# Opening modulation of a fused two-stage network: the 8 MiB matrix in two column halves, six buffers, its first product tiles started early, and later loads for other inputs

## The reference, cut to what matters

```python
def first_block(x, c, w_ada, b_ada, g_norm1, w_in, ...):
    ada = (c @ w_ada + b_ada)[:, None, :]               # c: (1, 1024), w_ada: (1024, 6144)
    shift1, scale1, gate1, shift2, scale2, gate2 = jnp.split(ada, 6, axis=-1)
    h = rmsnorm(x, g_norm1) * (1.0 + scale1) + shift1
    proj = h @ w_in                                     # all projections of the attention block
    (q_f, k_f, v_f, f_logit, q_d, k_d, v_d, q_i, k_i, w_i,
     gate_fox, gate_dsa) = jnp.split(proj, SPLIT_POINTS, axis=-1)
    log_f = jax.nn.log_sigmoid((f_logit + b_forget).astype(jnp.float32))
    cum_logf = jnp.cumsum(log_f, axis=1)
    ...                                                 # two attentions, gates, output product
    x = x + gate1 * (merged @ w_out)
    h2 = rmsnorm(x, g_norm2) * (1.0 + scale2) + shift2
    x = x + gate2 * (jnp.square(jax.nn.relu(h2 @ w_mlp1)) @ w_mlp2)
    return rmsnorm(x, g_final)
```

## Time and profile before

| what | value |
|---|---|
| median of three executions | 1395.11 us |
| the profiled execution | 1397.11 us |
| its span in the trace | 1395.4 us |
| TensorE busy | 1341.5 us, 96% of the span |
| VectorE, ScalarE, GpSimd busy | 823.8, 660.1, 79.6 us |
| read from HBM | 266.21 MB, 192 GB/s over the span |

### The profile page before, as it was taken

One profiled execution on the slowest core, in us unless ns is written; L12 is line 12 of the kernel. 1 busy time (PEld: TensorE's weight loads), 2 busy tenths in 40 slices (PEclk: granted clock), 3 DMA queues, 4 the chain that ended last, 5 costly groups with the idle time before them and its releaser, 6 DMA issues.

```text
span 1395.4 us, 16274 instructions
## 1 busy us (share of the span) xinstructions
PE 1341.5 (96%) x6233; PEld 1099.6 (79%) x6233; DVE 823.8 (59%) x1118; ACT 660.1 (47%) x1054; POOL 79.6 (6%) x114
## 2 busy tenths in 40 slices
PE   2999999999999999999989999999999999999997
PEld 2788877788888788888768888887888888888885
DVE  5686767867565654556437654557554575755454
ACT  2665555553444543445655443444443444544442
POOL 3400100100001000001001000000000010100000
PEclk9999999999999999999999999999999999999999
DMA  9766654458454655546424655557556555665551
GB/s 337 248 228 224 219 204 160 172 181 312 141 206 156 211 184 209 181 181 207 173 104 124 218 195 186 182 180 226 181 199 193 181 197 176 193 203 194 173 195 56
DMA packets 156717, 268.38 MB, mean 192 GB/s; under 512 B 9477, under 2 KB 101717, under 8 KB 155616
## 3 DMA queue, kind: packets, MB, share of 16 engines
q1 hardware_dynamic: 148896, 239.43, 50.3%
q0 software_dynamic: 7744, 27.91, 6.1%
HBM read 266.21 MB, written 1.07 MB: 192 GB/s over the span
## 4 chain that ended last, share of the span: by engine, by line
PE 87%; DVE 5%; DMA 3%; ACT 2%; POOL 1%; issue 1%; SPq 0%; DVEq 0%; ACTq 0%; POOLq 0%
PE UP L672 17%; PE UP L674 16%; PE UP L673 16%; PE Y L672 10%; PE Y L674 10%; PE Y L673 10%; PE TB L743 4%; DVE WL L1386 2%; DMA RAW<-in_w_in 1%; DMA X<-in_x 1%; POOL RS L599 1%; POOL VAR L598 1%; PE Y L773 1%; PE Y L780 1%; ACT WH L1047 1%
## 5 line engine op out<-in xcount | busy, mean ns | idle before, releaser
L1386 DVE TENSOR_TENSOR WL<-RAW,WH 128x1024 fp32r<-128x1024 f32 (+2 forms) x446 | 512.3, 1194 | 180.3 <-ACT WH L1047 174.1
L1047 ACT CAST WH<-RAW 128x1024 fp32r<-128x1024 f32 (+2 forms) x446 | 433.7, 1031 | 215.5 <-PE Y L674 126.1
L672 PE MATMUL UP<-WH,AH 128*128 128x512 f32 (+1 forms) x1120 | 452.0, 404 | 5.2 <-DVE WL L1386 3.3
L674 PE MATMUL UP<-WH,AL 128*128 128x512 f32 (+1 forms) x1120 | 437.9, 391 | 0.0
L673 PE MATMUL UP<-WL,AH 128*128 128x512 f32 (+1 forms) x1120 | 436.7, 390 | 0.0
L672 PEld LDWEIGHTS UP<-WH,AH 128*128 128x128 f32 x1120 | 211.3, 189 | 50.7 <-issue 8.5
L674 PEld LDWEIGHTS UP<-WH,AL 128*128 128x128 f32 x1120 | 210.9, 188 | 44.3
L673 PEld LDWEIGHTS UP<-WL,AH 128*128 128x128 f32 x1120 | 211.6, 189 | 39.6 <-issue 0.5
L672 PE MATMUL Y<-WH,HH 128*128 128x512 f32 (+1 forms) x496 | 193.8, 391 | 0.0
L674 PE MATMUL Y<-WH,HL 128*128 128x512 f32 (+1 forms) x496 | 191.8, 387 | 0.0
L673 PE MATMUL Y<-WL,HH 128*128 128x512 f32 (+1 forms) x496 | 191.7, 387 | 0.0
(11 more groups left out here) (213 smaller groups left out, 925.5 us busy)
## 6 DMA issues: line engine op xcount, KB each, us to landing
RAW<-in_ffn_w_gu SPq DMA_DIRECT2D x176, 512.0 KB, 5.0
RAW<-in_ffn_w_down SPq DMA_DIRECT2D x80, 512.0 KB, 4.1
RAW<-in_w_mlp SPq DMA_DIRECT2D x64, 512.0 KB, 4.2
RAW<-in_w_in SPq DMA_DIRECT2D x38, 512.0 KB, 5.9
PIECE<-in_w_ada POOLq DMA_DIRECT2D x32, 512.0 KB, 5.4
RAW<-in_a_w_in SPq DMA_DIRECT2D x24, 512.0 KB, 4.6
WADA<-in_w_ada SPq DMA_DIRECT2D x7, 1024.0 KB, 10.0
RAW<-in_w_out SPq DMA_DIRECT2D x8, 512.0 KB, 3.8
```

The lines of the kernel that those rows point to most:

```text
L672: pe.matmul(dst, ah, wh, start=first, stop=False)
L674: return pe.matmul(dst, al, wh, start=False, stop=last)
L1047: act.copy(WH[:, u % 2, q * n:(q + 1) * n], raw_half(u, q // 2)[:, (q % 2) * n:(q % 2 + 1) * n]).then_inc(wh_done, 1)
L1386: ve.tensor_tensor(WL[:, u % 2, o], raw_half(u, q // 2)[:, (q % 2) * n:(q % 2 + 1) * n], WH[:, u % 2, o].bitcast(F32), ALU.subtract).then_ ...
```

## The change

1. `w_ada` is loaded in column halves: a pair is two row blocks by 512 columns of shift and 512 of scale (two DMAs, 1 MiB). Four pairs make half 0, four half 1. Six places: the four of `WADA` and two in `ADA`. SP's order is now pair 0 of half 0, `x`, three pairs, unit 0, four pairs of half 1, unit 1. In the kernel before it was `w_ada` blocks 0 to 3, `x`, blocks 4 to 7, unit 0, unit 1.
2. ScalarE does the first product of each half (`opening_product`), VectorE adds the others in 512-column instructions, two for each row block, into `TG` (half 0) and `TMP` (half 1). The last two of half 1 are cut to 256 columns.
3. TensorE sums by quarters (two channel tiles), and unit 0 runs quarter by quarter for both token blocks (`first_unit`), into `Y[1]` instead of `UP`. Products whose result nobody reads stand between (`keep_busy`: 8, 6, 16 and 6 of 384 columns).
4. MOD of the first four tiles is written by ScalarE instead of VectorE.
5. The forget gate is formed once for both token blocks, after the second half of unit 1 is rounded; `lf_done` no longer frees the banks of unit 1, `scale_done` does.
6. VectorE's pieces of the later modulation are spread as (0, 1, 1, 2, 3, ...) instead of (2, 0, 1, 1, 3, ...), the sum still 24. GpSimd issues its first two pieces when unit 1 is split, and the table load after the fourth piece.

The core of the diff:

```diff
-MODULATION = (2, 0, 1, 1, 3, 3, 3, 3, 3, 3, 2)
+MODULATION = (0, 1, 1, 2, 3, 3, 3, 3, 3, 3, 2)
+ADA_SLOT = ((0, 1, 2, 3), (4, 5, 0, 1))
...
+        SPARE = ADA[:, :, :].rearrange("p (s a) n -> p s (a n)", s=2)
+        ACC = [buf[:, :, :].rearrange("p a n -> p (a n)") for buf in (TG, TMP)]
+        SUMB = [Y[0][0], Y[0][1], UP[0], UP[1]]
+        FIRST = Y[1]
...
             if k == "misc":
-                up_emptied.append((lf_done, tok + 1))
+                up_emptied.append((scale_done, 4))
...
-            for k in range(4):
-                sp.dma_start(WADA[:, k, :], wada[:, k, 0:2 * D]).then_inc(in_wada[k], 16)
-            sp.dma_start(X[:, :, :], t["x"][0].rearrange("(a p) n -> p a n", p=P)).then_inc(in_x, 16)
-            for k in range(4, KT):
-                sp.wait_ge(wada_used, k - 3)
...
+            def ada_pair(h, m):
+
+                for a in range(2):
+                    c = a * D + h * HALF
+                    sp.dma_start(ada_slot(h, m)[:, a * D:(a + 1) * D].rearrange("p (k n) -> p k n", k=2),
+                                 wada[:, 2 * m:2 * m + 2, c:c + HALF]).then_inc(in_wada[ADA_SLOT[h][m]], 16)
...
+            ada_pair(0, 0)
+            sp.dma_start(X[:, :, :], t["x"][0].rearrange("(a p) n -> p a n", p=P)).then_inc(in_x, 16)
+            for m in range(1, 4):
+                ada_pair(0, m)
+            load(0)
+            ada_pair(1, 0)
+            ada_pair(1, 1)
+            sp.wait_ge(acc_done, 2)
+            ada_pair(1, 2)
+            sp.wait_ge(acc_done, 6)
+            ada_pair(1, 3)
+            for u in range(1, len(UNITS)):
+                load(u)
...
                 gp.wait_ge(rev_out, 16 * (n + 1))
-                gp.wait_ge(wl_done, 6)
+                gp.wait_ge(wl_done, 12)
...
-            pieces(0, 2)
-            table_read(0)
...
-            pieces(2, 4)
+            gp.wait_ge(wl_done, 8)
+            pieces(0, 2)
...
+            pieces(2, 4)
+            table_read(0)
             pieces(4, PIECES + 2)
...
+            def keep_busy(n, unused):
+                for _ in range(n):
+                    pe.matmul(unused[:, 0:REV], IDR[:, :], CMR[:, :], start=True, stop=True)
...
+            ada_columns(0)
+            ada_columns(1)
+            keep_busy(6, FIRST[1])
+            first_unit(0)
+            first_unit(1)
             for h in range(2):
-                pe.wait_ge(*((acc_half, 1), (wada_used, KT))[h])
...
+                ready(("h", 1, h))
+            keep_busy(16, TB[0])
+            ada_columns(2)
+            ada_columns(3)
+            keep_busy(6, TB[0])
+            first_unit(2)
+            first_unit(3)
...
             round_unit(0, (0, 1))
-            mod_highs(0)
+            mod_highs(0, True)
+            opening_product(1)
+            mod_highs(1, True)
             round_unit(0, (2, 3))
-            mod_highs(1)
+            mod_highs(2, False)
+            mod_highs(3, False)
+            round_unit(1, (0, 1))
+            for tok in range(TOK):
+                act.wait_ge(mm_done, tok + 1)
...
+                act.copy(TMP[:, b % 2, 0:320], FIRST[tok][:, 0:320])
+                act.copy(TMP[:, b % 2, 320:384], FIRST[tok][:, 256:320]).then_inc(tmp_s, 1)
+            round_unit(1, (2, 3))
+            act.wait_ge(lf_in, 2)
+            step(act.activation(LF[:, :, 1, :], LF[:, :, 0, :], ACT.Abs))
```

More of the change, by code:

```diff
@@ L692, in wide @@
                 for k in range(kts):
-                    if u == 0 and tok == 0:
-                        pe.wait_ge(mod_low, k + 1)
                     if chain and k % 4 == 0:
@@ L1221, in _ @@
                     if tok == 0 and before == "misc":
-                        index_in(1)
+                        for n in range(TOK):
+                            index_in(n)
+                        round_unit(2, (2, 3))
                     elif tok == 0 and before in ("qf", "kf"):
@@ new lines, in accumulate @@
+            def accumulate(h, k, part=slice(0, HALF)):
+                ve.wait_ge(*ada_landed(h, k))
+                for a in range(2):
+                    if k == 1:
+                        ve.wait_ge(first_done, h + 1)
+                    else:
+                        ve.wait_ge(acc_done, sums[0] - 1)
+                    dst = ACC[h][:, a * HALF + part.start:a * HALF + part.stop]
+                    ve.scalar_tensor_tensor(dst, ada_row(h, k, a)[:, part], CC[:, k:k + 1], dst, ALU.mult, ALU.add
+                                            ).then_inc(acc_done, 1)
+                    sums[0] += 1
@@ new lines, in scales, with mod_whole @@
+            def scales(q):
+                k = 2 * q
+                ve.wait_ge(ada_done, q + 1)
+                ve.tensor_tensor(SHIFT[:, k:k + 2], SUMB[q][:, 0:2], COLS[:, k:k + 2], ALU.add)
+                for i in range(2):
+                    ins = ve.tensor_scalar(SCALE[:, k + i:k + i + 1], SUMB[q][:, 2 + i:3 + i], COLS[:, 8 + k + i:9 + k + i],
+                                           COLS[:, 16 + k + i:17 + k + i], ALU.add, ALU.mult)
+                ins.then_inc(scale_done, 1)
+            def mod_whole(q):
+                ve.wait_ge(scale_done, q + 1)
+                for k in (2 * q, 2 * q + 1):
@@ L1525, in modulated, with mod_lows @@
                     ve.tensor_scalar(MOD[:, k, :], XT[:, k, :], SCALE[:, k:k + 1], SHIFT[:, k:k + 1],
                                      ALU.mult, ALU.add).then_inc(mod_done, 1)
-            def mod_lows(first, end):
-                for k in range(first, end):
+            def mod_lows(q):
+                for k in (2 * q, 2 * q + 1):
                     ve.wait_ge(mod_done, k + 1)
@@ L1534, in mod_lows @@
                                      ).then_inc(mod_low, 1)
+            front, back = slice(0, 256), slice(256, HALF)
+            for k in range(1, KT):
+                accumulate(0, k)
+            scales(0)
             split_unit(0, (0,))
+            scales(1)
+            split_unit(0, (1,))
+            mod_lows(0)
+            for k in (1, 2, 3):
+                accumulate(1, k)
+            mod_lows(1)
+            for k in (4, 5):
+                accumulate(1, k)
+            split_unit(0, (2, 3))
+            accumulate(1, 6, front)
+            accumulate(1, 7, front)
+            accumulate(1, 6, back)
+            scales(2)
+            accumulate(1, 7, back)
             for h in (1, 3):
                 ve.wait_ge(*emptied(TURN[("h", 1, h // 2)]))
-            modulated(0)
-            mod_lows(0, 2)
-            split_unit(0, (1,))
-            mod_lows(2, 4)
-            split_unit(0, (2,))
-            modulated(1)
-            mod_lows(4, 6)
-            split_unit(0, (3,))
-            mod_lows(6, 8)
+            mod_whole(2)
+            scales(3)
+            mod_lows(2)
+            mod_whole(3)
+            mod_lows(3)
             piece = [0]
```

197 lines of the change are left out of this document (97 added, 100 removed).

## The result

| | before | after |
|---|---|---|
| median, us | 1395.54 (4 runs, 1394.97 to 1396.43) | 1403.3 (4 runs, 1402.16 to 1404.56) |
| profiled execution, us | 1397.1, span 1395.4 | 1404.56, span 1402.8 |

Ratio 1.005, 95% interval 1.0038 to 1.0062: the change costs about 7 us, where a gain of 2 was forecast. All times are medians of the fast executions: two of e6's twelve, of 3505 and 7569 us, are not counted.

What follows compares the result with a forecast made beforehand. TensorE's chain was taken to bound the kernel, movable only in the first hundred microseconds. Lead 3.5 less 1.3 (VectorE's piece) less 0.2 (moved loads) gave 2.0 us: 1393.1 from 1395.1; own range 1392.0 to 1394.6, 8 in 10 1390.9 to 1396.2.

Steps and rivals of the forecast that it cites:

- What bounds the kernel: Whole kernel: 87% of the chain that ended last is TensorE; only the first hundred microseconds can move the end.
- Prices on VectorE and loads of the opening: Opening: sums of 512 columns 0.66 us, half 0 done at 22.0, last low tile at 44.1.
- With quarters 1 and 2 in front I expect the fast pace by 37, and nothing is lost: Opening, useless products before the ones-products: TensorE's clock is fast by 37 us, costing nothing; TensorE leaves unit 0 at 46.0.
- rival (c): Opening: TensorE idles from about 40.3 to 42.3 and its clock falls, costing 4.8 us; 1397.9 us, chance 0.10.
- 3.5 us of lead: End of unit 1: block 1 ends at 57.8 us instead of 61.3, 3.5 us early.
- VectorE now adds one piece there, 1.28 us: Before unit 3's splits: an added piece leaves them 2.2 us early, at 68.7; the 3.5 us lead shrinks to 2.2.
- Shared out, 3.5 MiB from 82.4 at 3.0 us are done at 92.9 ... I take 0.2 us for it and keep 0 to 3: Unit 5's loads behind piece and table: landed at 92.9 us against 94.8 before; price 0.2 us, range 0 to 3.
- rival (b): Piece and table hold unit 5 by 2 to 3 us, or 2 KiB rows move slower: 1395 to 1396, chance 0.15.
- 217 GB/s: Moved table load: at this rate 1.5 MiB needs 7.2 us, losing 2 to 3; at 414 GB/s it needs 3.8.
- engines take turns between queues: Moved table load: by this rule it takes half of unit 5's rate while it lasts, making 2 to 3 us nearer.
- at least 1 MiB in a DMA: Opening loads cut to 512 KiB: no loss expected; by the page's 341 GB/s, 2 to 3 us worse.
- signs: Right: low tile 43 to 46, transposes 57 to 59, table near 80. Wrong: 0.28 spacing, unit 6 lead outside 1 to 3.

Runs made afterwards that it cites:

- e6: Kernel after, with ScalarE copying UP and PT before it rounds unit 5 in unit 4's block 0: 1399.44 us against 1397.44 for before, ratio 1.0014.
- e8: Kernel after, with the table load ahead of pieces 3 and 4 and without the opening's 16 and 6 useless products: ratio 1.0019 to before.
- e3: Kernel before, with only VectorE's modulation pieces spread as in after (0, 1, 1, 2): 1397.22 us, ratio 1.0007 to before.
- e1: Kernel after, with the 1 MiB table load issued ahead of pieces 3 and 4 instead of behind them: 1396.72 us against 1396.56 for before, ratio 1.0001.
- e2: Kernel before, with after's piece spread, pieces 3 and 4 issued as in after, and the table load behind piece 4: 1402.19 us, ratio 1.0042 to before.
- e4: Kernel after, with 26 useless products ahead of the values product in block 1 of unit 4: 1401.03 us, ratio 1.0031 to before.
- e7: Kernel after, table load ahead of pieces 3 and 4, opening's useless products 24, 8 and 12, UP and PT copied before unit 5's rounding: ratio 1.0001 to before.
- e5: Kernel after, table load ahead of pieces 3 and 4, opening's useless products 24, 8 and 12 instead of 16 and 6: ratio 0.9996 to before.

## Why the prediction was wrong

- **What bounds the kernel**: right. TensorE's chain, only the first 134 us decide, and the place named at L789/L816, its copy behind unit 5's rounding, is where the loss arose.
- **Prices on VectorE and loads of the opening**: nearly right, but not free. Sums 0.68 instead of 0.66, last low tile 45.7 instead of 44.1, inside the band of 43 to 46; the first low tile of quarter 3 is as late, and TensorE starts there.
- **"With quarters 1 and 2 in front I expect the fast pace by 37, and nothing is lost"**: failed. The 16 useless products ended at 38.2, but TensorE then idled for 1.20 and 1.41 us, and the clock was at half for the six useless products and three of quarter 3. TensorE left unit 0 at 49.12, not at 46.0. Of these 3.1 us VectorE's later chain makes 1.6, the useless products that stood in front of quarter 3 make 1.0, and the clock 0.5. It is rival (c)'s place, but not its cause in the main, and of the 3.5 us of lead 0.8 were left. How much the clock can cost there is shown by e8, which has no filling.
- **"VectorE now adds one piece there, 1.28 us"**: the duration was right, the cost at the end was 0.2 us (e3), within what can't be told from nothing. In e3 unit 5's second half was issued at 89.07, 1.3 us later than in before, but took 5.87 us instead of 7.03. In after the piece did shorten the lead: unit 3's split began at 71.43, after before's 70.94.
- **"Shared out, 3.5 MiB from 82.4 at 3.0 us are done at 92.9 ... I take 0.2 us for it and keep 0 to 3"**: this is the step that failed. Three things were mis-sized. VectorE was not early, so the load was issued at 88.23, not 85.5. It took 10.63 us, where I had judged by 3.5 MiB: the windows from 84 to 100 us move 4.8 MB, the 4.5 MiB of a piece, the table, both halves of unit 5 and two more pieces, issued at 92.55 and 93.88. In e1 these two are issued at 92.69 and 94.01 as well, but there the load has landed at 94.8; in after it landed at 98.9. And I treated the wait as its own price, while the fallen clock adds half as much again (e2: 2.6 us of wait and 1.6 of clock; e4 shows 2.7 us for the clock alone). The mechanism was in the text, as rival (b) with 2 to 3 us and 1395 to 1396; its true price in the profiled execution is 7.4 us, 4.8 + 2.6, where 0.2 was taken. e1 takes it away, and e2 puts it into before: 4.2 us of it in its fastest execution, 5.6 in the median. The same loads do not land at the same time in each execution: the second half's rounding begins at 98.95 in after, 97.21 in e4 and 96.97 in e2.
- **The rates taken from the earlier trace rows**: the 217 GB/s was read as the rate beside a piece. It is a queue with little in it: the piece was issued at 82.94, the first half of unit 5 at 85.07, and the second only at 87.75, inside that microsecond. From 91 to 93 us the same trace moves 375 to 385.
- The Trainium skill, page "DMA: Bandwidth & Descriptors", section "Queues, rings and completion order": its rule that engines take turns between queues was in the prediction as the reading that spoke against the change. The trace agrees in direction: with the table in the software queue the same load took 10.63 us and 8.67 (e2), without it 7.03, 6.63 (e1) and 5.87 (e3); that it is turns, and not only the bytes in front, no run here separates. The same page's rule, section "Rules for kernel authors", of at least 1 MiB in a DMA is borne out weakly: from 8 to 20 us, with `w_ada` in 512 KiB loads of 2 KiB rows, the loads move 386 GB/s, in before with 1 MiB loads of 8 KiB rows 412. That is 6% less, and no run separates the size from the row. The sums of half 0 ended at 23.0, where the prediction had 22.0. After, then before:

```profile
8.00:20.00 12.00, 6.85 (x24) 4.62 (x23) 6.54 (x10) 7.58 (x15) 3.21 (x5) 1.00 1.05 386
```

```profile
8.00:20.00 12.00, 1.45 (x2) 0.10 (x2) 8.34 (x4) 0.80 (x3) 0.00 (x0) 1.00 1.02 412
```

- The **signs**: of those on the side called right only the last low tile held (45.7). The transposes came at 61.12 (57 to 59), the table's load at 84.0 (near 80), the wait for L1188's copy was 5.4 us (1 to 3), and the second half landed at 98.9 (92 to 94). On the side called wrong two held: spacing at half pace in quarter 3, for three products, and TensorE at unit 6 less than 1 us early.

## What to carry to other kernels

- A load that is moved is priced at the place it moves to, by the next load of the critical engine behind it and by everything that stands in order behind the instruction that waits for that load. In before the second half of unit 5 was split by 98.3, 5.8 us before TensorE came to unit 5 (104.1), but for a small copy queued behind its rounding TensorE already waited 0.58 us.
- A wait of TensorE is priced with its clock: here 2.6 us more of it cost 4.2 (e2), and 4.8 more cost 7.4 (after).
- Useless products that hold the clock are work in front of work. In one lump ahead of the idle time they ended too soon to hold it; laid over the idle time they held it (1.00 at 44 to 46), but in two of three executions unit 1 then started later than with fewer of them (49.81 and 49.92 against 49.05), and in the third 0.7 us earlier.

## What the runs showed of the hardware

- The granted clock in the opening differs between executions of the same opening: at 34 to 36 us it was 1.00 in e7's and 0.50 in e5's, and the same 24 useless products ended 1.6 us apart. Of the nine profiled executions with the new opening it was 1.00 in two (after, e7) and 0.50 in seven.
- The clock column is not to be trusted alone early in the span: in after it reads 1.00 from 28 to 30 us, while the products there start 0.28 us apart, twice the 0.15 of those behind 33.7 us.
- Late in the kernel, behind a stretch where TensorE is busy for only about half of the time (in before 5.5 of 10 us, 720 to 730), the clock fell in eleven of the thirteen profiled executions; in e1's and e4's it did not. Before, then e1, 730 to 740:

```profile
730.00:740.00 10.00, 8.11 (x36) 6.68 (x35) 3.70 (x5) 5.42 (x11) 0.00 (x0) 0.66 0.00 0
```

```profile
730.00:740.00 10.00, 7.69 (x44) 6.18 (x43) 5.25 (x7) 7.04 (x12) 0.00 (x0) 1.00 0.01 2
```

With equal flips (133.79 and 133.78) the pooling products then start at 1160.9 and 1157.9. This 3 us, given or not, is as large as most effects in this study, and a single profile's span can't tell them; the marks before it can.
